# A decoder layer with 32 experts on one core: block turns on VectorE, a ring of 16 KB weight pieces, sums at the end, and another order in the sample attention

## The reference, cut to what matters

```
logits = h @ router_w + router_b;  top, eidx = top_k(logits, 4);  gates = softmax(top)
gu   = xb @ w_gu[e] + b_gu[e]                 # 1024 -> 2048
gate = min(gu[:, :1024], 7);  up = clip(gu[:, 1024:], -7, 7)
act  = gate * sigmoid(1.702 * gate) * (up + 1)
out  = act @ w_down[e] + b_down[e]            # 1024 -> 1024
x    = x + sum over the 4 experts of gates * out
```

## Time and profile before

| | us |
|---|---|
| three runs, median (range) | 2052.88 (2047.96 to 2056.23) |
| the profiled execution | 2053.49 |
| its span, first to last instruction | 2051.7 |
| TensorE busy | 1891.6 |
| VectorE, ScalarE, POOL busy | 465.1, 379.7, 342.5 |
| mean granted clock of TensorE | 0.946 |

### The profile page before, as it was taken

The page is one execution under the profiler, slowest core; times in us unless marked ns, Lnnn a source line. Parts: engine busy times, 40 slices in busy tenths (PEclk is TensorE's granted clock), DMA queues, the critical chain, the costliest instruction groups (busy, mean ns, idle before and its releaser), DMA issues.

```text
span 2051.7 us, 42512 instructions
## 1 busy us (share of the span) xinstructions
PE 1891.6 (92%) x17225; PEld 995.3 (49%) x17225; DVE 465.1 (23%) x1227; ACT 379.7 (19%) x854; POOL 342.5 (17%) x361
## 2 busy tenths in 40 slices
PE   7998987578799999959999999999999999999995
PEld 4447875354488885443343434343434343434342
DVE  2223334156411111152121212121111112121211
ACT  3232433145400000000111111111111111111110
POOL 0010001137400004100111111111212121212121
PEclk9998988599999999967999999999999999999997
DMA  8207524540241100019999999999999999999993
GB/s 294 84 19 258 196 75 192 237 147 1 83 144 52 62 21 16 31 36 412 392 397 394 395 394 398 393 398 389 400 392 397 393 398 395 397 393 395 395 395 113
DMA packets 106495, 532.03 MB, mean 259 GB/s; under 512 B 17640, under 2 KB 34800, under 8 KB 54737
## 3 DMA queue, kind: packets, MB, share of 16 engines
q1 hardware_dynamic: 85849, 469.42, 57.8%
q0 software_dynamic: 19824, 59.12, 10.1%
q10 hardware_dynamic: 768, 2.75, 0.3%
HBM read 508.82 MB, written 28.91 MB: 262 GB/s over the span
## 4 chain that ended last, share of the span: by engine, by line
PE 51%; DMA 2%; ACT 1%; issue 0%; DVE 0%; POOL 0%; POOLq 0%; DVEq 0%
PE psum L2593 30%; PE psum L2606 17%; PE psum L2579 1%; PE psum L2642 1%; PE psum L2587 1%; DMA arena<-scr_h,arena 1%; DMA y_sum<-arena 1%; PE psum L2632 1%; ACT arena L2517 1%; POOL y_sum L2488 0%; ACT arena L2522 0%; DVE arena L2544 0%; PE psum L2623 0%; DVE arena L2540 0%; ACT arena L2503 0%
## 5 line engine op out<-in xcount | busy, mean ns | idle before, releaser
L2593 PE MATMUL psum<-arena 128*32 128x512 f32 x6144 | 667.1, 591 | 0.0
L2593 PEld LDWEIGHTS psum<-arena 128*32 128x32 f32 x6144 | 201.6, 108 | 446.8 <-issue 441.0
L2606 PE MATMUL psum<-arena 128*32 128x256 f32 x6144 | 344.8, 379 | 8.1 <-ACT arena L2517 8.1
L2606 PEld LDWEIGHTS psum<-arena 128*32 128x32 f32 x6144 | 191.5, 109 | 143.6 <-ACT arena L2517 15.8
L2488 POOL DMA_INDIRECT y_sum<-arena x96 | 149.3, 1555 | 621.0 <-ACT arena L2522 615.0
L2558 DVE TENSOR_SCALAR arena<-psum 128x256 f32<-128x256 f32 x96 | 40.8, 425 | 883.4 <-PE psum L2593 880.7
L2282 PE MATMUL psum<-arena 128*128 128x272 f32 x768 | 182.3, 395 | 1.4 <-PEq L218 1.4
L2282 PEld LDWEIGHTS psum<-arena 128*128 128x128 f32 x768 | 146.6, 191 | 35.0 <-issue 3.1
L2514 ACT ACTIVATE arena<-arena 128x256 f32<-128x256 f32 x96 | 40.1, 418 | 610.8 <-DVE arena L2558 610.8
L739 PE MATMUL psum<-arena 128*128 128x512 f32 (+3 forms) x320 | 111.4, 507 | 0.2 <-DVE arena L611 0.2
L2522 ACT ACTIVATE arena<-psum,arena 128x256 f32<-128x256 f32 x96 | 45.2, 471 | 187.5 <-PE psum L2606 187.5
(11 more groups left out here) (350 smaller groups left out, 1579.8 us busy)
## 6 DMA issues: line engine op xcount, KB each, us to landing
arena<-in_w_gu SPq DMA_DIRECT2D x256, 1024.0 KB, 18.7
arena<-in_w_down SPq DMA_DIRECT2D x128, 1024.0 KB, 18.2
arena<-in_w_gb SPq DMA_DIRECT2D x24, 512.0 KB, 3.5
arena<-in_w_tok SPq DMA_DIRECT2D x3, 2048.0 KB, 10.3
arena<-in_x_all SPq DMA_DIRECT2D x8, 512.0 KB, 5.9
arena<-in_cache_mem SPq DMA_DIRECT2D x8, 512.0 KB, 10.5
arena<-in_cache_win SPq DMA_DIRECT2D x8, 512.0 KB, 7.2
arena<-in_w_up SPq DMA_DIRECT2D x1, 4096.0 KB, 12.8
```

The costliest lines, as they stand in the source:

```text
L2593: mm = pe.matmul(gu_bank(g)[32 * j:32 * j + 32].rearrange("p (h n) -> p h n", h=2), xgT[:, k, 32 * g:32 * g + 32], w_in_e[:, k, :, 256 * j ...
L2606: mm = pe.matmul(dn_half(g)[32 * j:32 * j + 32], actT[:, g, k % 2, 32 * (k // 2):32 * (k // 2) + 32], w_down_e[:, k, 256 * j:256 * j + 256 ...
```

## The change

**Expert phase.** (1) The host stores the expert weights so that a k tile takes 32 rows out of each quarter of the input channels, which lets 32x32 block turns stand in for full ones. `xg` is gathered as quarter rows (three gathers of 128 x 1 KB) and turned by one `dve.transpose` of 128x768; the activation is turned by a `dve.transpose` of 128x256 per group. TensorE's turns and the copies after them go; the norm's gain is multiplied in before `scr_h` is stored. (2) Weights go through a ring of nine 2 MB pieces, 16 KB per partition, six a block; SP runs one block ahead, and the first expert's pieces are loaded during merge and routing. Expert 0 always gets a block. (3) TensorE's loop body holds three blocks written out (the ring comes round after three), inside nested loops that leave early. (4) Pads point out of bounds, and gather and scatter skip them. (5) The scatter is a plain write to `y_of[k][token]`; at the end SP reads the four parts of every token back (8.9 MB), and VectorE (one addition of four by POOL) adds them and the biases to `x`.

**Sample attention.** Window rows get their own area for round 0 (the space of `hT`, which is spilled to HBM and read back in the next phase). Memory 0, window 0 and two of the gathers are issued a phase earlier. The order becomes M0, W0, S0 quarters 0 to 2, M1, S0 quarter 3, W1, S1.

```diff
@block.sync, expert phase
-                with sp.Fori(0, NBLK) as b:
-                    e = sp.value_load(e_row[0:1, bass.ds(b, 1)], min_val=0, max_val=NE - 1)
...
+                with sp.Fori(0, NBLK // 3) as i3:
+                    for u in range(3):
+                        with sp.If(3 * i3 + (u + 1) < blocks):
+                            e = sp.value_load(e_row[0:1, bass.ds(3 * i3 + (u + 1), 1)], min_val=0, max_val=NE - 1)
+                            for t in range(PER_BLOCK):
...
+                                sp.dma_start(ring[slot], weights(bass.ds(e, 1), t)).then_inc(e_in[slot], 16)
...
+                sp.wait_ge(e_y, blocks * G + G)
+                for n in ORDER:
+                    sp.dma_start(x_end(n)[0:ROWS[n]], scr_x[128 * n:128 * n + ROWS[n]]).then_inc(y_x, 16)
+                for g in range(G):
+                    sp.wait_ge(e_out[g], blocks * 16)
+                for n in ORDER:
+                    r = ROWS[n]
+                    sp.dma_start(four(n)[0:r, 0:2], y_of[0:2, 128 * n:128 * n + r].rearrange("k t n -> t k n")
+                                 ).then_inc(y_lo[n], 16)
@block.gpsimd
+                    for g in range(G):
+                        pool.sem_inc(e_sent, 1)
+                        pool.indirect_dma_start(xg[:, g], None, h_quarters, bass.IndirectOffsetOnAxis(row_from[:, g:g + 1], 0),
+                                                bounds_check=4 * NTOK - 1, oob_is_err=False).then_inc(e_g, 16)
...
+                                    pool.indirect_dma_start(y_quarters, bass.IndirectOffsetOnAxis(row_to[:, g:g + 1], 0),
+                                                            y_rows[:, g], None, bounds_check=4 * 1024 * TOPK - 1, oob_is_err=False
+                                                            ).then_inc(e_out[g], 16)
@block.vector
+                    dve.wait_ge(e_g, 16 * G * b + 16 * G)
+                    dve.transpose(xgT.rearrange("p g n -> p (g n)"), xg.rearrange("p g n -> p (g n)")).then_inc(e_xT, 1)
...
+                                    dve.transpose(actT[:, g], act_h[:, g]).then_inc(e_aT, 1)
...
+                        dve.wait_ge(p_bd, 2 * m + h + 1)
+                        sl = x_end(n)[0:r, 512 * h:512 * h + 512]
+                        dve.tensor_tensor(sl, bank((2 * m + h) % 6)[0:r], sl, ALU.add).then_inc(p_be, 1)
+                dve.wait_ge(p_be, 2 * NT)
...
+                    for k in range(2):
+                        link(dve.tensor_tensor(x_end(n)[0:r], x_end(n)[0:r], four(n)[0:r, k], ALU.add))
@block.tensor
-                        turn_tokens(b + 1)
-                        turn_act(b, 0)
-                        turn_act(b, 1)
-                        down(b, 0)
...
+                with pe.Fori(0, NBLK // 9) as nine:
+                    with pe.If(9 * nine < blocks):
+                        with pe.Fori(0, 3) as three:
+                            i3 = 3 * nine + three
+                            for u in range(3):
+                                b = 3 * i3 + u
+                                with pe.If(b < blocks):
...
+                                    for g in range(G):
+                                        down(b, g, i3, u)
@block.sync, merge and routing
+                early = PER_BLOCK // 2
+                for t in range(early):
+                    sp.dma_start(ring[t], weights(slice(0, 1), t)).then_inc(e_in[t], 16)
sample attention
-        BATCH = [(0, M, 0)] + [(0, S, q) for q in range(4)] + [(0, W_, 0), (1, M, 0), (1, W_, 0)] + [(1, S, q) for q in range(4)]
+        BATCH = ([(0, M, 0), (0, W_, 0)] + [(0, S, q) for q in range(3)] + [(1, M, 0), (0, S, 3), (1, W_, 0)]
+                 + [(1, S, q) for q in range(4)])
```

More of the change, by code:

```diff
@@ L937, in _ @@
                     load_memory(sp, 0, s)
+                sp.wait_ge(s_spill, 16)
+                for s in range(4):
+                    load_window(sp, 0, s)
                 sp.wait_ge(s_ct, 8 * 7)
@@ L1175, in _, with mask_blocks @@
                 blocks_of = lambda ap: ap.rearrange("p (a j k) -> p a j k", a=SUB, k=4)
[L1176 to L1184, removed]
+                def mask_blocks(r):
                     pool.wait_ge(d_pk, r + 1)
@@ L1188, in _ @@
                                        ALU.add).then_inc(d_sb, 1)
+                for s in range(2, 4):
+                    gather_selected(pool, 0, s)
+                mask_blocks(0)
+                filled(pool, 3, "wv", 0)
+                gather_selected(pool, 1, 0)
+                filled(pool, 2, "sv", 0)
+                for s in range(1, 4):
+                    gather_selected(pool, 1, s)
+                mask_blocks(1)
             def keys_out(eng, copy, n, mine):
@@ L1255, in _ @@
                 memory(0)
-                for n in range(1, 6):
+                keys(1)
+                window(0)
+                for n in range(2, 7):
                     keys(n)
+                memory(1)
                 selected(0)
-                window(0)
                 heads_out(0)
                 memory_out(0)
-                keys(6)
-                memory(1)
                 memory_out(1)
@@ L1429, in _ @@
                 importance(1)
+                keys(1)
+                window_max(0)
                 first_rows(0)
@@ L2014, in build_program @@
         bg = take(2048)
+        g2_row = take(D)
         assert cursor[0] <= tail_base + KD * D
@@ L2177, in _ @@
                 dve.memset(ones_b, 1.0)
-                dve.tensor_copy(before_b, before)
+                dve.tensor_scalar(at_least, iota32, -0.5, 0.5, ALU.add, ALU.min)
+                link(dve.tensor_copy(before_b, before))
                 residual(0)
@@ L2493, in _ @@
                     with pool.Else():
                         pool.nop()
-                pool.wait_ge(e_g, blocks * 16 + 16)
-                pool.nop().then_inc(e_all, 1)
+                pool.wait_ge(e_g, blocks * (16 * G) + 16 * G)
+                for m, n in enumerate(ORDER[:-1]):
+                    r = ROWS[n]
+                    pool.wait_ge(y_hi[n], 16)
+                    pool.tensor_tensor(four(n)[0:r, 2], four(n)[0:r, 2], four(n)[0:r, 3], ALU.add).then_inc(y_pair, 1)
             @block.scalar
@@ L2500, in _ @@
                 act.sem_inc(e_yc, G)
+                for n in range(NT):
+                    act.dma_start(scr_x[128 * n:128 * n + ROWS[n]], x[0:ROWS[n], n]).then_inc(p_x, 16)
+                blocks = used(act)
+                with act.Fori(0, NBLK // 9) as nine:
+                    with act.If(9 * nine < blocks):
+                        with act.Fori(0, 9) as one:
+                            b = 9 * nine + one
+                            with act.If(b < blocks):
+                                for g in range(G):
+                                    act.wait_ge(e_c, 2 * G * b + 2 * g + 1)
+                                    act.activation(act_h[:, g], gate_c[:, g], ACT.Sigmoid, scale=ALPHA).then_inc(e_sg, 1)
+                                act.wait_ge(e_ir, 2 * b + 2)
+                                for g in range(G):
+                                    act.wait_ge(e_y, G * b + G + g + 1)
+                                    act.activation(y_rows[:, g], dn_half(g), ACT.Copy, scale=cur_gate[:, g:g + 1]).then_inc(e_yc, 1)
+                                act.nop()
+                            with act.Else():
+                                act.nop()
+                    with act.Else():
+                        act.nop()
                 for n, (cols_n, b) in enumerate(((512, 7), (NTOK - 512, 6))):
```

615 lines of the change are left out of this document (315 added, 300 removed).

## The result

The changed kernel takes 2084.78 us (median of four runs, 2079.50 to 2086.36) where the kernel before takes 2051.32 in the runs beside it. The ratio is 1.0157, 95% interval 1.0128 to 1.0185. I had forecast 2022, faster. The profiled execution took 2079.50 us, its span is 2077.7: 26.0 longer than before.

A forecast was written before the change was run, and what follows sets the result against it. TensorE was taken to set the block period (33.95 us), with the DMAs nearly as close. From 2053.5 us, -62.4 + 30 - 8.5 + 22 + 8 - 20 = -30.9 gave 2022.6, or 2022 against the median; range 1975 to 2050.

The forecast's parts named there:

- Turns off TensorE: Expert blocks: removing TensorE's turns saves 1.95 us a block, -62.4 us over 32 blocks, if VectorE's turns stay hidden.
- The cover of 3.45 us: Expert block: VectorE is free for group 0 3.45 us before TensorE ends the third group, hiding its activation and turn.
- The loop of three blocks: TensorE's expert loop: the longer body does not stay loaded; ten jumps back at 3 us each add 30 us.
- The end: After the last product: leaving loops, bias products, VectorE's additions and store add 22 us, bounds +12 and +36.
- jumps over absent blocks: End of the expert loop: if these TensorE jumps each cost a fetch, 3 or so on the path add 8 us.
- The start: Before the first expert block: bias products move behind the loop, block 0 begins at 929 instead of 940; together -8.5 us.
- Sample attention: That phase: memory and window waits go, 7 us return through the clock, 4.5 of new wait; -20 us, bounds -8 and -25.
- A: Rival: TensorE's long body costs nothing, because it stays or the fetch comes in time; 1984 us, chance 0.25.
- C: Rival: 16 KB weight pieces make the DMAs set the period, slower than before; 2077 us at 34.8 a block, chance 0.09.
- the 7% read from the earlier trace: Weight DMAs: gathers of 16 KB rows ran 7% slower per byte than 8 KB pieces, but beside other work.
- A DMA share of 1.03 at 396 GB/s: Expert phase: read as DMAs at their limit beside TensorE, leaving no room; 0 to +2 us a block kept for the range.

The follow-up runs named there:

- experiments 6 and 7: Changed kernel with a two-block body and twelve 8 KB pieces: 2001.46 us; the same with the last two k done group by group as before: 1972.70 us.
- experiment 1: Changed kernel with a ring of six pieces in place of nine, TensorE's body kept at three blocks: 2078.73 us.
- experiments 3 and 7: Changed kernel, two-block body: six 16 KB pieces, 1970.35 us; twelve 8 KB pieces with the old order of the last two k, 1972.70 us.
- experiment 2: Changed kernel with a ring of six pieces and one block in TensorE's body: 1976.55 us.
- experiment 4: Kernel before the change with only TensorE's loop body written out to three blocks: 2179.10 us.

## Why the prediction was wrong, step by step

- **Turns off TensorE: right.** 31.62 us a block for a forecast of 31.9; with the mean of before, 33.95, the blocks gave back 1086.5 - 1011.8 = 74.7 us for a forecast of 62.4. VectorE's turn of 256 columns took 0.45 us, my value 0.42. The cover of 3.45 us was real and needed (experiments 6 and 7).
- **The loop of three blocks: the step that failed.** The mechanism and the count were right (ten jumps back, about ten pages a trip; by count a block of before has 820 records and not 826, and the new body 2376 and not 2394, which changes nothing in it); the size was not. "I take 3 us, near the idle landing" should have been 8.64: 3.58 for the fetch with little other traffic, 2.76 more because it stands in the weights' traffic, 2.0 for the clock that falls while TensorE stands still, and 0.3 over. My own text held the parts of the traffic and of the clock: it put a small landing in this traffic at 8 us against 3.8 in an idle queue, and the bias product at 1.47 us at the low clock for 0.83. I bounded one wait and left out what it does to the work behind it. That is 86.4 - 30 = 56.4 us of the 57.0 between the forecast and the profiled span. That nothing else seems to be missing is luck: the other four misses are of 2 to 12 us each and cancel to 0.7.
- **The end: under-sized by the same term.** The forecast gave 8 us to jumps over absent blocks; the stretch of 19.52 us falls to 4 (3.93 and 4.09) with a short body, so they cost 15.5. It was a term that I had named and priced at 3 us a jump here as well. The rest held: bias products 17.6, VectorE from 2054.64 to 2074.2, 19.6 for a forecast of 20.3.
- **The start: 6.6 us for 8.5.** The bias products went, but the gathers landed 10.4 us after issue and not 3.8, behind the three weight pieces that the ring of nine lets SP issue (6.3 us of TensorE's 19.04 wait, which is 12.72 in experiment 1). I had them landing as in an idle queue.
- **Sample attention: right where the change was made, and in the sum partly by luck.** Alone it gave -19.8 for a forecast of -20. The waits went; TensorE's 804 matmuls of the phase take 77.65 us for 85.47, 7.8 from the clock for the 7 forecast; the new wait on selected keys is 4.7 us in the changed kernel, 4 to 5 forecast. But the phase gave 23.2 and the prompt attention behind it took 3.7 back by its clock; the prediction had nothing for that.
- **Rivals.** A, "the long body costs nothing", was wrong of this kernel, but its 1984 is what a short body gives: 1976.55. C, the only rival on the right side, came within 8 us of the result by the wrong cause: 16 KB pieces are as good as 8 KB ones (queue 1 needs 2.41 us a MB with them and 2.43 with 8 KB pieces, experiments 3 and 7; the 7% read from the earlier trace rows did not hold). The case of a slower kernel through the jump itself was missing: -30.9 of the forecast, + 56.4 for the ten jumps, + 7.5 at the end, + 3.6 at the start, - 12.3 for blocks better than I had them and + 1.9 for the first one's clock are + 26.2, the measured sum.

## What to carry to other kernels

Before a loop body is written out longer, count the instructions of the engine that sets the pace: here a body of 1584 records ran without a fetch and one of 2376 paid 8.64 us at every jump back and 15.5 more on the way out, 102 us in all, more than all the rest of the change won (79 us, experiment 2). Where such a stall meets an engine with a clock of its own, add what its next work costs at the lower clock, and price a fetch in the traffic that it will meet. And where a ring of buffers forces a longer body, shorten the ring first: six pieces served at least as well as nine.

## What the runs showed of the hardware that I had not expected

- A DMA share of 1.03 at 396 GB/s was no limit. The same queues carried 415 GB/s at a share of 1.00 when TensorE asked for a block every 31.6 us, and the adding scatter still went in beside them.
- The clock falls on a short stop: 6.3 us, and even 3.6 us, of standing still brought products at the lower level (granted clock 0.50, bias product 1.47 us for 0.84), and the block behind took 2.0 to 2.2 us longer.
- A jump back costs the same kind of time where nothing is computed: with absent blocks only, TensorE's empty trips and their eleven pages held the program's end back (experiment 4). What each of them costs these traces don't show.
